# Who makes the gate's second one-hot: VectorE alone, four comparisons a group

## The reference

```python
def chunk_fn(xc):
    q = (xc @ wq).reshape(PEER_CHUNK, PEER_HEADS, 2, PEER_QDIM // 2)
    sc = jnp.einsum('thpd,pkd->thpk', q, subkeys)
    sv, si = lax.top_k(sc, PEER_TOPK)
    cand = sv[:, :, 0, :, None] + sv[:, :, 1, None, :]
    cv, ci = lax.top_k(cand.reshape(PEER_CHUNK, PEER_HEADS, PEER_TOPK * PEER_TOPK), PEER_TOPK)
    i1 = jnp.take_along_axis(si[:, :, 0], ci // PEER_TOPK, axis=-1)
    i2 = jnp.take_along_axis(si[:, :, 1], ci % PEER_TOPK, axis=-1)
    e = i1 * PEER_NKEYS + i2
    g = jax.nn.softmax(cv.astype(jnp.float32), axis=-1)
    act = jax.nn.gelu(jnp.einsum('td,thkd->thk', xc, u[e]))
    return jnp.einsum('thk,thkd->td', g * act, v[e])
```

## Time and profile before

| | |
|---|---|
| median of 3 runs | 1159.33 us |
| the profiled execution | 1160.83 us |
| its span, first to last instruction | 1159.0 us |
| TensorE matmul busy | 1099.8 us (95% of the span) |
| VectorE busy | 927.0 us (80%) |
| ScalarE busy | 659.3 us (57%) |
| GpSimd busy | 349.2 us (30%) |
| granted TensorE clock, mean | 0.994 |
| GpSimd L1528, 128 times | 144.5 us, mean 1129 ns |
| GpSimd L1543, 128 times | 136.2 us, mean 1065 ns |

### The profile page before, as it was taken

One profiled execution on the slowest core, in us unless ns is written; L12 is line 12 of the kernel. 1 busy time (PEld: TensorE's weight loads), 2 busy tenths in 40 slices (PEclk: granted clock), 3 DMA queues, 4 the chain that ended last, 5 costly groups with the idle time before them and its releaser, 6 DMA issues.

```text
span 1159.0 us, 21986 instructions
## 1 busy us (share of the span) xinstructions
PE 1099.8 (95%) x7174; PEld 978.3 (84%) x7174; DVE 927.0 (80%) x1701; ACT 659.3 (57%) x1042; POOL 349.2 (30%) x324
## 2 busy tenths in 40 slices
PE   6999999998999999999999999888888889999998
PEld 6688888888999999999999999666666667888887
DVE  5745666675899998889999999999999998444444
ACT  4254666664344444467777777666666665454453
POOL 0000222100001104643332333544544544545543
PEclk9999999998999999999999999999999999999999
DMA  7563222364545565544444444333443445555653
GB/s 255 163 228 129 73 74 74 115 194 147 167 145 170 179 193 182 186 155 165 152 157 163 162 154 156 120 135 127 135 136 127 134 137 186 195 189 191 198 186 122
DMA packets 50016, 181.34 MB, mean 156 GB/s; under 512 B 5552, under 2 KB 5680, under 8 KB 49968
## 3 DMA queue, kind: packets, MB, share of 16 engines
q1 hardware_dynamic: 49968, 180.72, 47.4%
HBM read 178.60 MB, written 2.10 MB: 156 GB/s over the span
## 4 chain that ended last, share of the span: by engine, by line
PE 51%; DVE 25%; issue 19%; ACT 2%; DVEq 2%; DMA 1%; POOL 0%; SPq 0%; ACTq 0%
PE bank L679 16%; DVE big L1436 7%; DVE gsum L1428 7%; DVE lo L1298 4%; PE bank L628 4%; PE bank L322 4%; PE bank L629 4%; PE bank L630 4%; PE bank L323 3%; PE bank L324 3%; PE bank L571 1%; DVE same L1410 1%; DMA raw<-wpre_d 1%; PE bank L336 1%; PE bank L338 1%
## 5 line engine op out<-in xcount | busy, mean ns | idle before, releaser
L925 ACT ACTIVATE hi<-raw 128x1024 fp32r<-128x1024 f32 x253 | 268.0, 1060 | 323.9 <-PE bank L679 172.6
L1298 DVE TENSOR_TENSOR lo<-raw,hi 128x1024 fp32r<-128x1024 f32 x253 | 315.3, 1251 | 105.7 <-ACT hi L925 104.9
L628 PE MATMUL bank<-xhi,hi 128*128 128x256 f32 x1024 | 293.6, 287 | 0.8 <-DVE lo L1298 0.8
L629 PE MATMUL bank<-xlo,hi 128*128 128x256 f32 x1024 | 289.5, 283 | 0.0
L630 PE MATMUL bank<-xhi,lo 128*128 128x256 f32 x1024 | 289.4, 283 | 0.0
L1543 POOL TENSOR_TENSOR auxl<-big,auxh 128x256 fp32r<-128x256 f32 x128 | 136.2, 1065 | 215.4 <-ACT auxh L947 215.4
L628 PEld LDWEIGHTS bank<-xhi,hi 128*128 128x128 f32 x1024 | 196.0, 191 | 2.2 <-issue 1.1
L629 PEld LDWEIGHTS bank<-xlo,hi 128*128 128x128 f32 x1024 | 196.3, 192 | 0.0
L630 PEld LDWEIGHTS bank<-xhi,lo 128*128 128x128 f32 x1024 | 196.0, 191 | 0.0
L1528 POOL TENSOR_TENSOR oneB<-kep,eT 128x512 fp32r<-128x512 f32 x128 | 144.5, 1129 | 156.4 <-PE bank L642 146.9
L679 PE MATMUL bank<-hi,auxh 128*128 128x512 f32 x508 | 161.2, 398 | 3.2 <-ACT hi L925 2.8
(11 more groups left out here) (234 smaller groups left out, 1752.8 us busy)
## 6 DMA issues: line engine op xcount, KB each, us to landing
raw<-u_d SPq DMA_DIRECT2D x128, 512.0 KB, 3.3
raw<-v_d SPq DMA_DIRECT2D x128, 512.0 KB, 3.3
raw<-wpre_d SPq DMA_DIRECT2D x78, 512.0 KB, 4.0
big<-x_d SPq DMA_DIRECT2D x2, 512.0 KB, 3.8
out_d<-big SPq DMA_DIRECT2D x2, 512.0 KB, 5.1
big<-out_d SPq DMA_DIRECT2D x2, 512.0 KB, 4.9
out_d<-big SPq DMA_DIRECT2D x4, 256.0 KB, 2.1
big<-cst_d SPq DMA_DIRECT2D x1, 719.5 KB, 7.3
```

The lines of the kernel that those rows point to most:

```text
L628: pe.matmul(out, wh, xhi[:, k, :], start=(k == 0), stop=False)
L629: pe.matmul(out, wh, xlo[:, k, :], start=False, stop=False)
L925: act.activation(hi[:, n % SPLIT, :], raw[:, n % RING, :], ACT.Copy).then_inc(hi_done, 1)
L1298: dve.tensor_tensor(lo[:, n % SPLIT, :], raw[:, n % RING, :], hi[:, n % SPLIT, :].bitcast(F32), ALU.subtract).then_inc(lo_done, 1)
```

## The change

GpSimd's `distances` and ScalarE's two activations a group are gone. VectorE makes `oneB` with four `tensor_scalar` instructions a group, each 128x128: is_equal of 0 to 127 with one number per partition, i2 of that token. They stand behind `rows_a` of the same group. GpSimd's queue holds only `w_lo` in this part of the program.

```diff
 ScalarE
-            def one_hot_b(i, j, base):
-
-                g = base + j
-                act.wait_ge(S("dist"), i * UNROLL + (g + 1))
-                B = oneB[:, g % 2, :, :].bitcast(F32)
-                act.activation(oneB[:, g % 2, :, :], B, ACT.Square).then_inc(S("dist_sq"), 1)
-                act.wait_ge(S("dist_sq"), i * UNROLL + (g + 1))
-                act.activation(oneB[:, g % 2, :, :], B, ACT.Relu, bias=1.0,
-                               scale=-1.0).then_inc(S("oneB_ready"), 1)
...
             def u_step_g(i, j):
-                one_hot_b(i, j, 1)
                 loop_hi(i, N_PRE + HALF + j + SPLIT)
                 gelu_pair(i, j, HALF)
...
             def v_step_g(i, j):
-                one_hot_b(i, j, NGRP + 2)
                 loop_hi(i, V0 + j + SPLIT)
                 w_hi(i, j + SPLIT)
...
 VectorE
+            def one_hot_b(i, j, base):
+
+                g = base + j
+                if g >= 2:
+                    dve.wait_ge(S("g_ready"), i * UNROLL + (g - 1))
+                for t in range(4):
+                    i2 = eT[:, 1, bass.ds(i * (4 * UNROLL) + (4 * (g % NGRP) + t), 1)]
+                    m = dve.tensor_scalar(oneB[:, g % 2, t, :], iota, i2, None, ALU.is_equal)
+                m.then_inc(S("oneB_ready"), 1)
+
...
             rows_a(0, 0, 0)
+            one_hot_b(0, 0, 0)
             keys_equal(0, 2, 0)
             rows_a(0, 1, 0)
+            one_hot_b(0, 1, 0)
...
                 weigh(i, j, base)
                 if rows:
                     rows_a(i, j, base + 2)
+                    one_hot_b(i, j, base + 2)
...
 GpSimd
-            def distances(i, j, base):
-
-                g = base + j
-                if g >= 2:
-                    pool.wait_ge(S("g_ready"), i * UNROLL + (g - 1))
-                i2 = eT[:, 1, bass.ds(i * (4 * UNROLL) + 4 * (g % NGRP), 4)].unsqueeze(2).broadcast_to([P, 4, P])
-                pool.tensor_tensor(oneB[:, g % 2, :, :], iota.unsqueeze(1).broadcast_to([P, 4, P]), i2,
-                                   ALU.subtract).then_inc(S("dist"), 1)
...
-            def v_step_g(i, j):
-                distances(i, j, NGRP + 3)
-                w_lo(i, SPLIT + j)
...
+            each_tile(pool, NBLK, lambda i, j: w_lo(i, j))
```

More of the change, by code:

```diff
@@ L969, in _ @@
             act.activation(gw2[:, :, 0], eT[:, 2, :], ACT.Copy).then_inc(S("gw2_hi"), 1)
-            one_hot_b(0, 0, 0)
             for j in range(ROUTER, HALF):
@@ L973, in _ @@
             each_tile(act, HALF - 1, u_step_g)
-            one_hot_b(0, 0, NGRP)
             act.wait_ge(S("weighed"), 1 + NGRP)
@@ L991, in _ @@
                 w_hi(0, b)
-            one_hot_b(0, 1, NGRP)
             each_tile(act, HALF - SPLIT, v_step_g)
-            one_hot_b(0, HALF - 1, NGRP)
             loop_hi(0, V0 + HALF)
```

## The result

The changed kernel takes 1191.47 us (median of 4 runs, 1190.01 to 1193.7) against 1159.25 us for the kernel before (4 runs): ratio 1.0278, 95% interval 1.0259 to 1.0297, so 32 us slower. The prediction said 1189.7 us and a range of 1172 to 1206. The span of the profiled execution went from 1159.0 to 1190.1 us, +31.1.

The account below looks back on a forecast made before the run. VectorE was taken as full in both stretches, with TensorE also full in U. U +31.4, V -1.8 and the end +0.8 sum to +30.4 us, giving 1189.7 us against the median 1159.33; range 1172 to 1206.

Parts of the forecast that it names:

- The comparison's price: One 128x128 comparison on VectorE, 0.20 us from start to start; four a group make 0.80 us.
- Rivals 1 (0.144): In both stretches, a comparison costs only 0.144 us: U +17.4, V -8.4, 1169 us in all; chance 0.06.
- 2 (0.267): In both stretches, a comparison costs 0.267 us, by type or address computation: U +48.4, V +6.6, 1215 us; chance 0.09.
- U: Stretch with groups 0 to 63: VectorE becomes the bound alone, 3.81 us a step against TensorE's 3.31; +31.4 us.
- GpSimd's hold: In U, `keys_equal` on VectorE waits for GpSimd's `distances`, 0.30 us of each 3.31 us step; the change frees it.
- rival 4: The hold of `keys_equal` in U is not GpSimd's and stays 0.30: U 4.11 a step, 1208 us; chance 0.04.
- V: Stretch with groups 65 to 125: 3.94 us a step instead of 3.97 over 60 steps; -1.8 us.
- The chain through `w_lo`: In V, ScalarE's high part releases `w_lo`, which holds `keys_equal` for 0.13 us a step, delaying `weigh`: 3.94 a step.
- Rival 3: V gives back more than U costs, comparison at 0.144, `w_lo` holding nothing: V -23.0, U +17.4, 1154 us; chance 0.03.
- p: VectorE's time for one 128-column comparison, taken as 0.20 us; 0.01 us of it was said to be worth 5 us.
- The hand-over: Between `add_parts` 63 and 65, from U to V: VectorE's gaps cover the comparisons' 0.8 us; counted as zero.
- The last group: At the end, group 127's comparisons put the last group 0.8 us later; TensorE's last 65 tiles run as before; +0.8 us.

## Why the prediction was right

**The comparison's price**, the term on which the sum hung, was taken from six scalings of another stage: 0.20 us each, 0.80 for four. Measured 0.78 to 0.79, also in fp32r and with a shifted address. Rivals 1 (0.144) and 2 (0.267) fell with that. The cheaper figure, 0.142 us as estimated from the Trainium skill (Vector Engine (DVE) Microarchitecture Reference, 5.2), is not what a comparison with a number per partition takes here: the measurement decides, 0.195. The Trainium skill's rule on many small tiles (VectorE: DVE Perf Modes, the section on the TRN2 errata) held: one wide instruction at 0.60 against four at 0.78, although the four are quicker by the column (0.5 ns in the earlier trace rows against 1.04).

**U.** VectorE's own work was read as 3.01 us by taking the 0.30 us of GpSimd's hold out; forecast 3.81 a step, measured 3.79, +30.1 us where +31.4 was said. That the hold was spare and not lost is shown by the run without a one-hot (3.30 a step), and its end by `keys_equal` at 0.33, so rival 4 fell.

**V.** The chain through `w_lo` was forecast at 3.94 and measured at 3.94 (-1.8 us both). It is shown, not only fitted: 3.53 without comparisons (3.55 said), 3.735 with two (3.75), 3.85 with the wide one (3.85), 3.80 with `w_lo` released sooner (3.81). It holds where `w_lo` runs into `keys_equal`; with ScalarE alone it did not, and V went below it, to 3.39. Rival 3, V giving back more than U costs, failed at both of its conditions. Its limit was not worked out rightly: with 3.01 + 4p in both stages the times are equal at p = 0.154, and faster by 0.2% below 0.150, not 0.147. Nor is p by 0.01 us worth 5 us under the forecast's own chain, in which a comparison counts half in V: it is 3.7. Neither moves the forecast.

**The hand-over** was the step that failed in size: counted as zero, because VectorE had gaps there. It had, but the comparisons fell on GpSimd's first `w_lo`, for which TensorE waits, and the clock came back later: +2.0 us, of which 1.4 went when the comparisons were moved out of the way. The last group is 0.8 us later, as said (`add_parts` 127 lies 5.78 us behind 125 instead of 4.99), but what follows it is 0.4 shorter, so the term came to +0.4.

The sum missed by 0.7 us in the span (+30.4 against +31.1), which is luck in part: the U term's 1.3 us too much and the hand-over's 2.0 too little stand against each other.

## What to carry to other kernels

An engine that the profile shows as full may be partly held, and what it is held by is seen only from start to start, with the other engine's instructions laid beside. Work taken off the engine that holds is worth what the next chain leaves of it: of the 0.84 us of `weigh` in V 0.44 came without any one-hot, and 0.58 with ScalarE alone, where the engines fell into another arrangement. Work put on the full engine counts wholly where that engine alone sets the step (U), and by half where it is part of a chain over two steps (V). Give each stage its own division of labour: V gained with ScalarE doing the one-hot alone, U lost with the same.

## What the runs showed of the hardware

- A tensor_scalar of 128x128 with one number per partition and a GpSimd tensor_tensor stretch each other: four went from 0.78 to 1.04 us, the GpSimd instruction from 0.72 to 1.22.
- An activation of 128x128 with a bias per partition takes 0.32 us on ScalarE, so that four cost 1.29 us where one of 128x512 costs some 0.65.
- In U of the changed kernel's profile VectorE's durations grow, from 0.69 us of `add_parts` at 518 us to 0.81 at 757, while they stay at 0.67 to 0.69 in the other profiles, where the starts lie as far apart (3.79 us a step in both of the other runs with four comparisons in U). The longer duration is real for whoever waits for the end: TensorE's weight load of the gate starts 1.05 us behind the first comparison (652.90, 653.95), and 0.93 in the run with group 65's comparisons moved; the first `w_hi` starts 0.58 behind its `weigh` instead of 0.44. It costs no step where VectorE itself is the bound. What makes it grow, no run here tells.
